# Bidirectional scans: how the sum of the two directions is split between TensorE and GpSimd

## The reference

```python
cb = jnp.einsum('bclgn,bcsgn->bclsg', Cc, Bc)
y_diag = jnp.einsum('bclsge,bcsgep->bclgep', cb[..., None] * decay, X)
y_off = jnp.einsum('bclgn,bcgepn->bclgep', Cc, s_in) * jnp.exp(a_cs)[..., None]
...
y_bwd = flip(ssd_chunked(flip(xs), flip(dt[:, :, 1]), a[1], flip(bm), flip(cm)))
y = y_fwd + y_bwd + d_skip.astype(f32)[:, None] * xs
```

## Time and profile before

| | us |
|---|---|
| median of the runs | 1672.0 (1670.74 to 1673.18) |
| span of the profiled execution, first to last instruction | 1670.3 |
| PE busy | 1643.4 |
| DVE busy | 990.2 |
| POOL busy | 674.2 |
| ACT busy | 662.7 |

### The profile page before, as it was taken

The page is one execution under the profiler, slowest core; times in us unless marked ns, Lnnn a source line. Parts: engine busy times, 40 slices in busy tenths (PEclk is TensorE's granted clock), DMA queues, the critical chain, the costliest instruction groups (busy, mean ns, idle before and its releaser), DMA issues.

```text
span 1670.3 us, 20403 instructions
## 1 busy us (share of the span) xinstructions
PE 1643.4 (98%) x7924; PEld 1303.3 (78%) x7924; DVE 990.2 (59%) x1560; ACT 662.7 (40%) x916; POOL 674.2 (40%) x339
## 2 busy tenths in 40 slices
PE   7999999999999999999999999999999999999999
PEld 5777778877878888878877777787878788887887
DVE  4589869787755444522237898697877544454000
ACT  5455552335343333322244555523444433333121
POOL 3332223233445555544444222223234555555443
PEclk9999999999999999999999999999999999999999
DMA  5532134352222222222223221354522232322223
GB/s 169 140 96 76 51 111 145 133 145 92 92 95 91 96 93 96 94 79 95 91 89 126 86 73 64 121 145 132 146 94 89 89 101 88 101 89 98 82 92 107
DMA packets 56415, 170.93 MB, mean 102 GB/s; under 512 B 5792, under 2 KB 10656, under 8 KB 56320
## 3 DMA queue, kind: packets, MB, share of 16 engines
q1 hardware_dynamic: 55936, 168.88, 31.5%
q0 software_dynamic: 384, 0.75, 0.4%
HBM read 166.24 MB, written 3.38 MB: 102 GB/s over the span
## 4 chain that ended last, share of the span: by engine, by line
PE 91%; DMA 2%; issue 2%; POOL 2%; ACT 2%; DVE 1%; SPq 0%; DVEq 0%; ACTq 0%; POOLq 0%
PE banks L1145 27%; PE banks L1147 26%; PE banks L1146 26%; PE banks L1244 2%; PE banks L1223 2%; PE banks L1232 2%; DMA sb_w_raw<-w_out 2%; PE banks L1298 1%; PE banks L1311 1%; PE banks L1203 1%; PE banks L1325 1%; POOL sb_xc L465 0%; DMA sb_x_stream<-x_t 0%; PE banks L1282 0%; ACT sb_w_hi L520 0%
## 5 line engine op out<-in xcount | busy, mean ns | idle before, releaser
L425 POOL TENSOR_TENSOR sb_w_lo<-sb_w_raw,sb_w_hi 128x1024 fp32r<-128x1024 f32 x200 | 482.4, 2412 | 645.8 <-ACT sb_w_hi L520 645.8
L1145 PE MATMUL banks<-sb_h_hi,sb_w_hi 128*128 128x512 f32 x1344 | 550.8, 410 | 12.3 <-POOL sb_w_lo L425 10.9
L520 ACT ACTIVATE sb_w_hi<-sb_w_raw 128x1024 fp32r<-128x1024 f32 x256 | 270.9, 1058 | 720.3 <-PE banks L1147 702.8
L1147 PE MATMUL banks<-sb_h_hi,sb_w_lo 128*128 128x512 f32 x1344 | 530.9, 395 | 0.0
L1146 PE MATMUL banks<-sb_h_lo,sb_w_hi 128*128 128x512 f32 x1344 | 530.4, 395 | 0.0
L1145 PEld LDWEIGHTS banks<-sb_h_hi,sb_w_hi 128*128 128x128 f32 x1344 | 253.4, 189 | 93.8 <-issue 34.8
L1146 PEld LDWEIGHTS banks<-sb_h_lo,sb_w_hi 128*128 128x128 f32 x1344 | 253.8, 189 | 60.7 <-issue 6.5
L1147 PEld LDWEIGHTS banks<-sb_h_hi,sb_w_lo 128*128 128x128 f32 x1344 | 253.3, 188 | 59.4
L1110 DVE TENSOR_TENSOR banks<-banks,sb_rstd 128x512 f32<-128x512 f32 x88 | 61.6, 699 | 145.2 <-PE banks L1147 135.7
L1145 PE MATMUL banks<-sb_ff_hi,sb_w_hi 128*128 128x512 f32 x352 | 140.6, 399 | 6.8 <-DVE sb_ff_val L1113 6.8
L1146 PE MATMUL banks<-sb_ff_lo,sb_w_hi 128*128 128x512 f32 x352 | 140.3, 399 | 0.0
(11 more groups left out here) (204 smaller groups left out, 2267.8 us busy)
## 6 DMA issues: line engine op xcount, KB each, us to landing
sb_w_raw<-w_in SPq DMA_DIRECT2D x88, 512.0 KB, 3.4
sb_w_raw<-w_up SPq DMA_DIRECT2D x88, 512.0 KB, 3.3
sb_w_raw<-w_out SPq DMA_DIRECT2D x32, 512.0 KB, 3.3
sb_w_raw<-w_down SPq DMA_DIRECT2D x32, 512.0 KB, 3.3
sb_e<-sum_rows SPq DMA_DIRECT2D x16, 512.0 KB, 5.9
sb_bias_t<-bias_rows SPq DMA_DIRECT2D x16, 448.0 KB, 6.2
sb_exp_cs<-sum_rows SPq DMA_DIRECT2D x32, 192.0 KB
sb_w_raw<-w_down SPq DMA_DIRECT2D x16, 384.0 KB, 3.0
```

What stands on the lines that cost most here:

```text
L425: g.tensor_tensor(WLO[:, n % 2, :], W[:, n % 2, :], WHI[:, n % 2, :].bitcast(F32), ALU.subtract).then_inc(w_lo.handle, 1)
L520: sc.activation(WHI[:, n % 2, :], W[:, n % 2, :], ACT.Copy).then_inc(w_hi.handle, 1)
L1145: mm(out, whi, hhi, start=start, stop=False)
L1147: return mm(out, wlo, hhi, start=False, stop=stop)
```

## The change

An even head no longer has its directions added by GpSimd over all four chunks, and an odd head by TensorE over all four. Now GpSimd adds two chunks of every head (`one_sum`: chunks 2 and 3 of an even head, 0 and 1 of an odd one), and TensorE adds the other two by accumulating two products. `gs_done` counts to 16 per layer instead of 8. In `within`, the products that need no sum come first, in alternating halves, then a wait for the sums of both heads, then the four products with a sum. The wait for `gs_done` at the head of the block is gone. The lines of the file move: L456 is L462, L460 is L466, L465 is L471, L481 is L487, L1311 is L1310, L1325 is L1338.

```diff
-    gs_done = sem("gs_done", SSD_HEADS // 2)
+    gs_done = sem("gs_done", SSD_HEADS)
...
+    def one_sum(h):
+
+        first = (QT // 2) * (1 - h % 2)
+        return slice(P * first, P * (first + QT // 2))
...
         def add_directions(h):
 
+            at = one_sum(h)
             pool.wait_ge(*g_done.at(h + 1))
-            g.tensor_tensor(head_e(h)[:, 0, :], head_e(h)[:, 0, :], head_e(h)[:, 1, :], ALU.add).then_inc(gs_done.handle, 1)
+            g.tensor_tensor(head_e(h)[:, 0, at], head_e(h)[:, 0, at], head_e(h)[:, 1, at], ALU.add).then_inc(gs_done.handle, 1)
...
-                if s in WEIGH_AT and WEIGH_AT[s] % 2 == 0:
+                if s in WEIGH_AT:
                     add_directions(WEIGH_AT[s])
...
         def within(t):
 
-            pe.wait_ge(*gs_done.at(t + 1))
+            def product(h, c, d, last):
+                half = 64 * (h % 2)
+                return mm(BANK[half:half + 64, 6 + t % 2, P * c:P * c + P], XT[:, c, 64 * (h % 8):64 * (h % 8) + 64],
+                          head_e(h)[:, d, P * c:P * c + P], start=d == 0, stop=last)
+
             pe.wait_ge(*g_done.at(2 * t + 2))
...
-            for c in range(QT):
-                for h, d in ((2 * t, 0), (2 * t + 1, 0), (2 * t + 1, 1)):
-                    half = 64 * (h % 2)
-                    ins = mm(BANK[half:half + 64, 6 + t % 2, P * c:P * c + P], XT[:, c, 64 * (h % 8):64 * (h % 8) + 64],
-                             head_e(h)[:, d, P * c:P * c + P], start=d == 0, stop=d == h % 2)
-                    if c == QT - 1 and d == h % 2:
+            for i in range(QT // 2):
+                for d in range(2):
+                    product(2 * t, i, d, d == 1)
+                    product(2 * t + 1, QT // 2 + i, d, d == 1)
+            pe.wait_ge(*gs_done.at(2 * t + 2))
+            for i in range(QT // 2):
+                for h in (2 * t, 2 * t + 1):
+                    ins = product(h, i + one_sum(h).start // P, 0, True)
+                    if i == QT // 2 - 1:
                         ins.then_inc(y_mm.handle, 1)
```

## The result

The changed kernel takes 1680.3 us (median of 5 runs, 1678.9 to 1682.6) beside 1671.7 us for the kernel before (5 runs, 1670.7 to 1673.2). The ratio is 1.0050, with a 95% interval of 1.0039 to 1.0061: **8.6 us slower**, where 6.3 us were forecast. The profiled execution has a span of 1678.7 us, 8.4 more than before.

A forecast was written before the change was run, and what follows sets the result against it. TensorE, busy 98% of the span, was taken as the bound, VectorE nearly limiting in the scans. Layer 0's +3.7 and layer 1's +2.6 gave +6.3 us: 1676.6 against the profiled span, 1678.3 for the runs; range 1671.0 to 1684.0.

The forecast's parts named there:

- The saving: TensorE's 16 `within` blocks, one per head pair and layer: 1.90 to 1.46 us, 0.44 less each, 7.0 in all.
- The overlap of the halves: In a block, even and odd heads' products run beside each other on the array's column halves; 7.0 us rests on it.
- Rival 4: Blocks on TensorE: halves don't overlap, nothing saved, waits remain; +10.3 us, 1682.3; chance 3%.
- The add: GpSimd's 256-column add: 0.74 us alone, bounds 0.65 and 1.30; the odd head's is needed 0.9 us into the block.
- rival 3: GpSimd's add has mostly fixed cost (1.30 us) and holds VectorE off; +11.7 us, 1683.7; chance 12%.
- Pair 0: Layer 0, first block: add behind `ml_sc` and VectorE's split ends near 267.05; wait 1.4 us, shift +1.0.
- Pairs 1 and 2: Layer 0, next two blocks: adds in time, no wait; -0.44 us each, to +0.1 on TensorE.
- Pair 3: Layer 0: +0.6 us at block start, wait 3.1, shift +3.3; layer 1: wait 2.0 instead.
- Pairs 4 to 7 and the tail: Layer 0: pairs 4 to 6 -0.44 us each, pair 7 waits 0.8, shift +3.2; with the gate, +3.7.
- The wait for the late weights: TensorE's z tile wait at 371.41 moves with block 4, to +2.8 us; savings of pairs 5 and 6 are lost.
- the second gate: GpSimd's gate of pair 6 (L465) now stands behind head 15's add, beside a split: 0 to 1.3 us, 0.5 added.

The follow-up runs named there:

- tensor_all: Changed kernel with no adds by GpSimd; TensorE does all 16 products of every block: 1672.1 us.
- filled: Changed kernel, but at pair 3 TensorE repeats the block's first eight products (four times in layer 0, three in layer 1) instead of idling: 1677.2 us.
- no_odd_add: Changed kernel without GpSimd's adds for odd heads and the wait for them, leaving part of the sum out: 1667.8 us.
- late_pair0: Changed kernel with GpSimd's low part of the short-convolution mix in slot 5 computed three times, delaying head 1's add: 1685.8 us.
- gate_only: Changed kernel with GpSimd's gate of pair 6 put ahead of its add of head 15 in slot 22: 1679.3 us.
- gate_first: add_first with GpSimd's gate of pair 6 put ahead of its add of head 15 in slot 22: 1672.1 us.
- add_first: Changed kernel with GpSimd's adds of heads 1 and 7 put ahead of `ml_sc` in slots 5 and 11: 1671.0 us.
- hybrid_0237: Changed kernel in pairs 1, 4, 5 and 6; division by head of the kernel before in pairs 0, 2, 3 and 7: 1670.5 us.
- alone_37_mid: add_first, TensorE doing all products in pairs 3 and 7; elsewhere products from the states moved between first eight products and add wait: 1671.7 us.

## Why the prediction was right, and which terms were off

**The saving.** 0.44 us a block is right: unblocked blocks take 1.46 us (pair 5: 368.59 to 370.05). The overlap of the halves, against which a rule of the Trainium skill ("TensorE: Matmul & The Clock Gate", Part 3) was held, is settled by tensor_all: 32 passes in the time of 24. The measurement goes against what I drew from that rule. Rival 4 falls.

**The add.** 0.74 us for 256 columns was measured at 0.73, and beside a split at 1.64 to 1.73: rival 3, a mostly fixed cost, falls. (Its words give VectorE "as much again" as 2.2 us a layer, its sum 0.5; the outcome does not hang on it.) That the second to ask starts when the first ends holds too. The Trainium skill, "SBUF — State Buffer", "Who interferes with whom", puts it as one shared lock, given in order of asking and held for the whole instruction, and the order at 311.91 and 311.99 agrees.

**Pair 0.** The add was expected to end near 267.05 and ended at 267.13. The wait was 0.7 us and not 1.4 because TensorE itself came 0.7 us later, which it already was ahead of the scans, where nothing is changed. The end of the block hangs on the add alone, so the shift behind it, +1.1, is the +1.0 forecast all the same.

**Pairs 1 and 2.** Pair 1 as forecast. Pair 2 waited 0.5 us in layer 0, where none was priced. VectorE's split there began 1.6 us later than before, TensorE 0.65, and the add behind it, asked for at 294.43, took 1.64. VectorE was late because ScalarE's wait for the weights of the earlier trace rows had grown from 1.12 us:

```profile
284.90 1.06 ACT L526 ACTIVATE sb_w_hi<-sb_w_raw 128x1024 fp32r<-128x1024 f32 x1 [2.51 <-DMA sb_w_raw<-w_in]
```

In filled, the same code up to there, that wait was 1.08 us and pair 2 had none. The landing of that load varied by 1.4 us between two executions, more than this term.

**Pair 3.** +0.6 was forecast at the start of the block and +3.3 behind it, +0.8 and +3.9 were measured; the wait of 3.0 us is the 3.1 forecast, and layer 1's 2.0 is 2.0. The failed term is what comes behind: *a wait was priced at its own length*. Behind it the clock was at half, which made the last four products 0.4 us longer in layer 0 and the tile products 2.0 and 1.5 us, 3.9 us in all. That is the term missing from the sum.

**Pairs 4 to 7 and the tail.** The wait for the late weights moves with block 4, as forecast, and takes back half of pair 5's saving. At pair 7 the wait inside the block was 0.7 as against 0.8, but the wait at its start shrank by 0.7, since the add of head 15 keeps the second gate away from VectorE's segments (3.46 us). I had seen that the gate moves, and priced only its later place, at 0.5; its move gave 0.7 back at pair 7. The 1.0 us at the sum of squares in each layer, against that 0.5, is a lost race: in the traces of all 12 kernels the tree's first add takes 2.4 us where it starts before the split and 3.4 where it starts behind it. That the moved gate alone made it lose is not shown, since no_odd_add loses it too.

The sum was 6.3. With the clock's 3.9 it would have been 10.2; the traces give 8.4, so the other terms together were some 2 us too pessimistic. That 6.3 came so near to 8.6 is thus in part luck: a missing cost and terms set too high made up for each other. The mechanism of the waits is not luck, for the wait inside pair 3 came out right in both layers. By filled, the change without the fall of the clock would still lose about 5 us.

## What to carry to other kernels

Before giving work to a second engine to balance a third one, look at what stands in front of it in that engine's queue at the moment of need: here two queue positions were worth 9 us, and the balanced block at most 4. A wait of some microseconds on TensorE is not priced by its length alone; read PEclk in the stretch behind it. And check what an existing split between engines saves at all: the 16 adds of the kernel before saved nothing, because the block was as long as its longer half.

## What was unexpected of the hardware

- The granted clock fell to half behind idle times of 3.0 us (layer 0) and 2.0 us (layer 1, with another 1.2 us ahead of the block) inside pair 3, and of 4.3 us in late_pair0; the work behind the wait then ran at half clock for 3.4 to 6.2 us. It did not fall behind 1.9 us at pair 3 of late_pair0, and behind the same 1.6 us and 0.75 us around pair 7 it fell in gate_only and not in gate_first. The idle time alone does not tell; what else does was not tried.
- Such falls also come without the change. The kernel before has two, one in the feed-forward part of each layer, and each costs it about 1.6 us. Every kernel here waits 3.4 us for VectorE at both places; in the traces of add_first, no_odd_add and hybrid_0237 only one of the two falls came. That is part of why runs of one kernel lie 2 to 3 us apart, and why a trace's span has to be held beside the median. The one of layer 1:

```profile
1542.40:1545.70 3.30, 3.30 (x9) 2.56 (x9) 0.87 (x2) 0.00 (x0) 1.27 (x1) 0.50 0.49 159
```

- Changing between products of 128 and of 64 columns costs 0.34 us more for each further change and back (alone_37_mid, ten blocks), though the products of 64 keep their spacing.
